# The front of a recurrence unit reordered, and gates computed two units ahead

## The reference, cut to what matters

```python
def step(S, inp):
    w_t, k_t, v_t, kk_t, a_t = inp[:5]
    sa = jnp.einsum('bhvk,bhk->bhv', S, -kk_t)
    S = (S * w_t[:, :, None, :] + sa[..., None] * (kk_t * a_t)[:, :, None, :]
         + v_t[..., None] * k_t[:, :, None, :])
    y = jnp.einsum('bhvk,bhk->bhv', S, inp[5])
```

```python
mu = jnp.mean(wkv, axis=-1, keepdims=True)
var = jnp.mean(jnp.square(wkv - mu), axis=-1, keepdims=True)
gn = ((wkv - mu) * lax.rsqrt(var + GN_EPS)).reshape(B, T, H * N) * ln_g + ln_b
bonus = sum(jnp.sum(r * k_d * r_k, axis=-1, keepdims=True) for k_d in k_dirs) * v
out = (gn + bonus.reshape(B, T, H * N)) * g
```

## Time and profile before

| | us |
|---|---|
| median of 3 runs | 4013.6 (4007.03 to 4015.18) |
| profiled execution, its own time | 4013.55 |
| its span | 4011.7 |
| TensorE busy | 3545.7 (88%) |
| VectorE busy | 1615.0 (40%) |
| ScalarE busy | 1021.3 (25%) |
| GpSimd busy | 1036.3 (26%) |
| mean granted TensorE clock | 0.919 |

### The profile page before, as it was taken

The page is one execution under the profiler, slowest core; times in us unless marked ns, Lnnn a source line. Parts: engine busy times, 40 slices in busy tenths (PEclk is TensorE's granted clock), DMA queues, the critical chain, the costliest instruction groups (busy, mean ns, idle before and its releaser), DMA issues.

```text
span 4011.7 us, 76327 instructions
## 1 busy us (share of the span) xinstructions
PE 3545.7 (88%) x33290; PEld 2603.9 (65%) x33290; DVE 1615.0 (40%) x2806; ACT 1021.3 (25%) x1590; POOL 1036.3 (26%) x664
## 2 busy tenths in 40 slices
PE   8997698879878899989999989859999999979997
PEld 3454477623325677768888855428888888857885
DVE  3255641311126755434333340305555555623333
ACT  2032232211114244331111021312333333223221
POOL 0002341121213200033222120015444444324441
PEclk9997899889988999989999989978889989989998
DMA  4206143169971100111111113420000000012221
GB/s 174 94 32 280 60 181 156 75 258 357 372 280 37 43 1 1 51 77 74 64 63 64 64 59 128 170 93 3 13 13 14 13 14 14 3 64 78 101 95 42
DMA packets 64569, 378.85 MB, mean 94 GB/s; under 512 B 12906, under 2 KB 12906, under 8 KB 26352
## 3 DMA queue, kind: packets, MB, share of 16 engines
q1 hardware_dynamic: 40032, 291.52, 18.7%
q0 software_dynamic: 20608, 68.82, 4.5%
q10 hardware_dynamic: 3600, 13.63, 0.9%
HBM read 380.21 MB, written 44.04 MB: 106 GB/s over the span
## 4 chain that ended last, share of the span: by engine, by line
PE 75%; DVE 10%; DMA 6%; ACT 4%; issue 3%; POOL 2%; SPq 0%; DVEq 0%; ACTq 0%; POOLq 0%
PE psum L462 20%; PE psum L474 11%; PE psum L475 10%; PE psum L476 10%; PE psum L750 4%; DMA arena<-in_wall 3%; PE psum L2096 2%; DVE arena L3146 2%; PE psum L769 2%; PE psum L2123 2%; DMA ring<-in_wall 1%; PE psum L648 1%; PE psum L2814 1%; PE psum L2797 1%; DVE arena L3364 1%
## 5 line engine op out<-in xcount | busy, mean ns | idle before, releaser
L462 PE MATMUL psum<-arena 64*64 64x64 f32 (+3 forms) x13256 | 623.2, 241 | 58.9 <-POOL arena L3049 21.2
L462 PEld LDWEIGHTS psum<-arena 64*64 64x64 f32 (+2 forms) x13256 | 501.1, 143 | 161.9 <-issue 116.5
L492 POOL TENSOR_TENSOR ring_low<-ring,slab_high 128x2048 fp32r<-128x2048 f32 x66 | 303.9, 4618 | 647.5 <-ACT slab_high L485 647.3
L474 PE MATMUL psum<-h_high,slab_high 128*128 128x512 f32 (+1 forms) x1056 | 378.2, 358 | 16.5 <-DVE h_low L512 10.0
L475 PE MATMUL psum<-h_low,slab_high 128*128 128x512 f32 (+1 forms) x1056 | 377.0, 357 | 0.0
L476 PE MATMUL psum<-h_high,ring_low 128*128 128x512 f32 (+1 forms) x1056 | 376.5, 357 | 0.0
L462 PE MATMUL psum<-arena,ring 128*128 128x512 f32 (+3 forms) x992 | 370.4, 533 | 1.8 <-DVEq L1269 1.0
L462 PEld LDWEIGHTS psum<-arena,ring 128*128 128x128 f32 (+2 forms) x992 | 184.8, 187 | 185.4 <-issue 174.9
L941 DVE TENSOR_TENSOR arena<-arena,psum 128x512 f32<-128x512 f32 x66 | 39.5, 599 | 486.1 <-PE psum L476 481.9
L474 PEld LDWEIGHTS psum<-h_high,slab_high 128*128 128x128 f32 x1056 | 201.3, 191 | 51.8 <-issue 10.7
L476 PEld LDWEIGHTS psum<-h_high,ring_low 128*128 128x128 f32 x1056 | 201.6, 191 | 28.5
(11 more groups left out here) (433 smaller groups left out, 6116.0 us busy)
## 6 DMA issues: line engine op xcount, KB each, us to landing
ring<-in_wall SPq DMA_DIRECT2D x181, 1024.0 KB, 5.1
arena<-in_wall SPq DMA_DIRECT2D x96, 1024.0 KB, 12.0
moe_rows<-arena POOLq DMA_DIRECT2D x2, 6144.0 KB, 67.5
arena<-moe_rows ACTq DMA_DIRECT2D x24, 512.0 KB, 7.6
moe_out<-arena POOLq DMA_DIRECT2D x24, 512.0 KB, 9.0
arena<-spill POOLq DMA_DIRECT2D x8, 1024.0 KB, 5.2
spill<-arena POOLq DMA_DIRECT2D x2, 3072.0 KB, 17.6
filters<-arena POOLq DMA_DIRECT2D x2, 2048.0 KB, 6.6
```

Source lines behind the costliest of these rows:

```text
L462: last = L.eng.matmul(out, a, b, start=(i == 0), stop=(i == len(pairs) - 1))
L474: L.eng.matmul(out, a_hi, b_hi, start=(i == 0), stop=False)
L492: L.eng.tensor_tensor(m.low[:, n % SLOTS, :], m.ring[:, n % SLOTS, :], m.high_of(n).bitcast(F32), ALU.subtract).then_inc(m.sem("slab_split ...
```

## The change

- `around` also gives `later`, unit n + 2. Its gates, products and sigmoids, are issued in unit n: on TensorE behind the solved values and ahead of the features products, on ScalarE behind the copies of the solved values. The gates of unit 1 are issued ahead of unit 0. `sigmoid_ready_scalar`, one sigmoid of a single column, stands ahead of those copies.
- A chain step stands behind each operand's six transposes, three in all, and the readout of the states behind the first of the two akv groups.
- The readout of the pair before moves behind corner products: mean in the first level, sums of squares in the second, bonus in the third, turn and gate in the fourth. VectorE centres in the first level, takes the reciprocal in the second, scales in the fourth and ends in the fifth. `readout_tensor` is parted into `readout_sums_tensor` and `readout_bonus_tensor`, and VectorE's bonus product, now `readout_bonus_vector`, stands right behind the scan.
- VectorE's reciprocal of the removal norm moves behind the first chain step of the turns, its two transposes of the inverse ahead of the states' readout.

```diff
-def unit_tensor(L, m, B, u, before, done, after, w2, g2):
-    if after is not None:
-        gates_tensor(L, m, B, after, w2)
+def unit_tensor(L, m, B, u, before, done, after, later, w2, g2):
...
     for k, src in enumerate((u.al, u.be, u.ka)):
-        for half, tiles in enumerate(TURNS):
+        for tiles in TURNS:
             turned.append(turn_pair_tensor(L, m, src, tiles))
-            if before is not None and k < 2:
-                chain_tensor(L, m, B, before, FIRST + 2 * k + half)
-    if done is not None:
-        readout_mean_tensor(L, m, B)
+        if before is not None:
+            chain_tensor(L, m, B, before, FIRST + k)
...
     for hh in range(2):
         L.eng.wait_ge(*akt[hh])
         turned.append(squares_tensor(L, hh, lambda *at: [(square(B.akt, *at), tok(B.vtok, *at))]))
-    if done is not None:
-        readout_tensor(L, m, B, done, g2)
+        if before is not None and hh == 0:
+            chain_tensor(L, m, B, before, ALLCH - 1)
...
         if done is not None and lv == LEVELS[0]:
+            readout_mean_tensor(L, m, B)
+        if done is not None and lv == LEVELS[1]:
+            readout_sums_tensor(L, m, B)
+        if done is not None and lv == LEVELS[2]:
+            readout_bonus_tensor(L, m, done)
+        if done is not None and lv == LEVELS[3]:
             readout_turn_tensor(L, m, B)
-        if done is not None and lv == LEVELS[1]:
             readout_gate_tensor(L, m, B, done, g2)
...
         solved.append(squares_tensor(L, hh, lambda *at: [(square(B.tt, *at), square(B.akv, *at))]))
+    if later is not None:
+        gates_tensor(L, m, B, later, w2)
     for solution in solved:
         L.eng.wait_ge(*solution)
```

ScalarE:

```diff
+def sigmoid_ready_scalar(L, m):
+
+    L.eng.activation(m.stat[:, 20:21], m.tab("gn_eps"), ACT.Sigmoid).then_inc(L.step, 1)
+    L.eng.wait_ge(L.step, L.next_step())
...
-    if after is not None:
-        gates_scalar(L, m, B, after)
...
         if done is not None and lv == LEVELS[0]:
+            L.next_bank()
+            readout_squares_scalar(L, m, B)
+        if done is not None and lv == LEVELS[1]:
+            readout_root_scalar(L, m, B)
+        if done is not None and lv == LEVELS[2]:
             readout_spread_scalar(L, m, B)
...
     if after is not None:
         decay_exp_scalar(L, m, B, after)
+    if later is not None:
+        sigmoid_ready_scalar(L, m)
     for hh in range(2):
         for dst in (B.ua, B.uv):
             ps = L.next_bank()
             L.eng.wait_ge(L.bank_full, L.fill)
             copy(of_head(dst, hh), tiled(ps[:, :TT * CH]), -1.0)
+    if later is not None:
+        gates_scalar(L, m, B, later)
```

VectorE:

```diff
+        chain(FIRST + k)
+        if k == 0 and after is not None and after.d == 0:
+            removal_inverse_vector(L, m, removal_rooted)
     turned_back = []
     for hh in range(2):
         L.eng.wait_ge(m.sem("inverse_begun"), L.nth("inverse_begun"))
         turned_back.append(inverse_turn_vector(L, m, B.ti, B.tt, hh))
-    if after is not None and after.d == 0:
-        removal_inverse_vector(L, m, removal_rooted)
+    L.next_bank()
+    chain(ALLCH - 1)
+    L.next_bank()
     if after is not None:
         decay_scan_vector(L, m, B, after)
     if done is not None:
-        readout_centre_vector(L, m, B, done)
-    L.next_bank()
-    L.next_bank()
-    if done is not None:
-        readout_inverse_vector(L, m, B)
-        bonus = L.next_bank(), L.bank_full, L.fill, L.bank_free, L.read_out
+        readout_bonus_vector(L, m, done)
...
         if done is not None and lv == LEVELS[0]:
+            readout_centre_vector(L, m, B)
+        if done is not None and lv == LEVELS[1]:
+            readout_inverse_vector(L, m, B)
+        if done is not None and lv == LEVELS[2]:
+            bonus = L.next_bank(), L.bank_full, L.fill, L.bank_free, L.read_out
+        if done is not None and lv == LEVELS[3]:
             terms = readout_scale_vector(L, m, B, done, bonus)
-        if done is not None and lv == LEVELS[1]:
-            readout_vector(L, m, B, done, terms)
+            gate = L.next_bank(), L.bank_full, L.fill, L.bank_free, L.read_out
+        if done is not None and lv == LEVELS[4]:
+            readout_vector(L, m, B, done, terms, gate)
```

More of the change, by code:

```diff
@@ L3256, in unit_scalar @@
         copy(of_head(B.akv, hh), tiled(ps[:, :TT * CH]), 1.0)
-    if done is not None:
-        readout_root_scalar(L, m, B)
+        if before is not None and hh == 0:
+            L.next_bank()
     if after is not None and after.d == 0:
@@ L3277, in unit_scalar, with unit_vector @@
             copy(of_head(dst, hh), tiled(ps[:, :TT * CH]), -1.0)
+    if later is not None:
+        gates_scalar(L, m, B, later)
     for _ in range(8):
         L.next_bank()
-def unit_vector(L, m, B, u, before, done, after):
+def unit_vector(L, m, B, u, before, done, after, later):
     e = L.eng
@@ L3328, in unit_vector @@
     for k in range(3):
-        for half in range(2):
-            L.next_bank()
-            if k < 2:
-                chain(FIRST + 2 * k + half)
+        L.next_bank()
+        L.next_bank()
+        chain(FIRST + k)
+        if k == 0 and after is not None and after.d == 0:
+            removal_inverse_vector(L, m, removal_rooted)
     turned_back = []
@@ L3369, in unit_vector @@
         L.next_bank()
+    if later is not None:
+        L.next_bank(2)
+        L.next_bank(2)
     ecol = u.ecol.rearrange("q (t p) -> q t p", p=2)
@@ L3404, in readout_tensor @@
         L.eng.wait_ge(bank_free, count)
-    L.eng.matmul(ps, ones, u.bk, start=True, stop=True).then_inc(L.bank_full, 1)
+    L.eng.matmul(ps, m.tab("heads64"), u.bk, start=True, stop=True).then_inc(L.bank_full, 1)
 def readout_gate_tensor(L, m, B, u, g2):
@@ L3492, in around @@
     u = unit(n)
[L3493 removed]
+    return u, unit(n - 1), (unit(n - 1) if u.d == 0 else None), unit(n + 1), unit(n + 2)
 def recurrence_tensor(L, m, B, w2, g2):
     prepare_tensor(L, m, B, Unit(B, 0), w2)
+    gates_tensor(L, m, B, Unit(B, 1), w2)
     for n in range(UNITS):
@@ L3552, in recurrence_vector @@
     terms = readout_scale_vector(L, m, B, last, bonus)
-    readout_vector(L, m, B, last, terms)
+    gate = L.next_bank(), L.bank_full, L.fill, L.bank_free, L.read_out
+    readout_vector(L, m, B, last, terms, gate)
 def build(nc, a):
```

45 lines of the change are left out of this document (23 added, 22 removed).

## The result

The changed kernel takes 3956.8 us in the median of 4 runs (3951.7 to 3957.6), the kernel before in the same comparison 4011.7: a ratio of 0.9868, 95% interval 0.9848 to 0.9887. The profiled execution has a span of 3955.8 us against 4011.7. The sign was right and so were most of the steps; the size was not, and the term that was most too small is the clock's.

The account below looks back on a forecast made before the run. TensorE was taken as the bound, with only its idle time and clock to win. Waits removed -35.9, new waits +17.5, mask waits -2 and clock -6 gave -26 us: 4013.6 to 3988 us, range 3962 to 4014.

Parts of the forecast that it names:

- Gates: Behind the solved values, units 0 to 13: gates cover TensorE's 0.79 us wait for ScalarE's copies; 11.0 us gained.
- step 2: Scores: TensorE's waits for PSUM banks that gates hold until the sigmoids read them go; 2.5 us of 4.3 gained.
- Readout squares: Readout sums: TensorE's seven waits for ScalarE's square go, as sums stand a level behind the mean; 10.9 us gained.
- spread: Odd units: TensorE's wait for the removal norm's spread goes, as its reciprocal moves up on VectorE; 3.5 us gained.
- Chain in the turns: Turns: six transposes behind every chain step remove hidden waits, 0.55 us a unit; 8 us gained over 15 units.
- Bonus product: First corner level, even units: VectorE's product, issued ahead of GpSimd, takes 0.75 us; TensorE idles 0.35 us for masks.
- Sums in the second level: Second corner level, even units: VectorE stands still for the reciprocal ahead of updates; TensorE idles 0.55 us a unit.
- Last part of readout: Fifth level, even units: two VectorE operations delay the solved values 0.7 us, a GpSimd operand product 0.7 us more.
- The clock: First corner of four even units: the half-speed spell behind the 1.55 us wait goes; 6 us gained.
- the clock steadies: Rival, units 1 to 14: 50 of 132 us at half speed go, another 15 us gained, 3973; chance 0.15.
- the clock takes it back: Rival, turns: runs of transposes lengthen the low stretch 3.4 us in 15 units, 16 us lost, 4009; chance 0.17.
- VectorE as the bound of the even levels: Rival, five levels of seven even units: inserted VectorE operations uncovered, 8.7 us a unit, 4037; chance 0.12.

Follow-up runs that it names:

- gates-alone kernel: Kernel before with only the gates moved two units ahead, chain and readout left in place: ratio 0.9922 to the kernel before.
- chain-alone kernel: Kernel before with only chain steps, states' readout and the removal norm's reciprocal moved: ratio 0.9977 to the kernel before.
- the parts alone: Kernel before with one part of the change each: gates 0.9922, chain 0.9977, readout 0.9988.
- the fourteen kernels: The changed kernel and all follow-up variants, each timed beside the kernel before: ratios 0.9754 to 0.9958.
- with the product added: Changed kernel with three VectorE waits moved (0.9823), plus one unread 128x512 product ahead of the removal norm's twelve narrow sums in odd units: 0.9812.
- without the gates: Changed kernel with the gates put back at the head of the unit before: ratio 0.9950 to the kernel before.
- before with wide sums: Kernel before with the removal norm's twelve narrow sums replaced by one 128x512 product, norm not computed rightly: ratio 0.9958.

## Why the prediction was wrong

By its steps:

- *Gates* (11.0 us): right for the waits listed. L462's wait for ScalarE is 1.6 us in two units instead of 11.8 in fifteen, and in the gates-alone kernel idle time fell by 14.6 us, with the bank waits of step 2 (2.5) in it. At full speed that kernel is 22 us shorter, though: 8 us more lay under modelled ends, which neither step counted.
- *Readout squares* (10.9) and *spread* (3.5): right. Neither wait is in the list after.
- *Chain in the turns* (8 us under modelled ends): right in size. The chain-alone kernel, which has the spread's 3.5 us in it as well, is 12 us shorter at full speed where 11.5 were reckoned. But it was the only step with hidden waits, and in the changed kernel there are some 20 us of them.
- *Bonus product*: right in mechanism. It is issued behind the scan and takes 0.73 us in the median, not 1.87; GpSimd's first copy waits for it (0.63 us where it took 0.2). Mask wait 0.77 us against 0.35 reckoned.
- *Sums in the second level* (0.55): 0.61 measured, by the very path named: sums, table load, reciprocal, update.
- *Last part of readout* (0.7 + 0.7): too small. Over the program L3501 takes 2.126 us in the median and 0.752 at least. The wait for GpSimd was 1.4 us, not a mean of 0.7, in every unit but the tail, since the two engines stand in the same order each time; TensorE lost 2.4 to 2.6 us, not 1.4. A collision in a fixed schedule has no average: it is to be priced by the place where the two meet, or at both ends.
- Together the visible idle time was to fall by 12 us (35.9 - 8 + 2 - 17.5) and fell by 5.9.
- *The clock* (6 us): this is the step that failed. "With the wait gone I count 6 us gained" looked at one stretch in four even units, 14 us at half speed. Between the two traces 82 us went, from 136.6 to 54.6, worth 29 us at 0.35 each; over all executions 57 us, worth 20. I took the long stretches in the front as given and put their shortening into a rival. That rival, "the clock steadies" (50 us more at 0.31 each, 15 us on top of the 6), has both the amount and the price nearly right, and it had a chance of 0.15 only. It gave 3973. Of the 16 us from there to 3957, 8 are waits that no step had, 2 the lower median of the kernel before in this comparison, and 6 lie within the interval of the ratio.

Forecast and result side by side, units 1 to 14 (the same sum from the other side):

| | forecast | in the two traces |
|---|---|---|
| visible idle time | -12 | -6 |
| waits under modelled ends | -8 | -22 |
| clock | -6 | -29 |
| sum | -26 | -57 |

With the half-speed time of all executions the clock's line is -20 and the sum -48, where the ratio says -53 (interval -61 to -45). Which waits beside the chain's lay under modelled ends stays open: none is long enough to be listed, and no run parted them further.

The rival by which the clock takes it back is refuted: half-speed time fell, and the front of unit 6 runs its longest row of transposes at 1.00. The Trainium skill, TensorE: Matmul & The Clock Gate ("Part 4: PE-mode transpose"), says that transpose-mode matmuls don't count as busy time for the clock gate in the same way. If so, it was no bar here: twelve of them in a row, 1.53 us amid chain steps and scores without waits, didn't lower the clock. VectorE as the bound of the even levels did not come either, but its price shows: (21.6 + 5.4) / 7 = 3.9 us of new waits in an even unit, of the 5.4 at which it would have decided, and the even units gained less than the odd ones. That the readout's move is worth nothing by itself (0.9988 alone, 0.9880 without it against 0.9868 with it) is this rival's share.

## What to carry to other kernels

Where TensorE is 93% busy, look at the granted clock of the stretch beside its idle time: small waits and narrow products cost once by their length and again by the half-speed stretch that follows. Price a us at half speed from units of one kernel that do the same work (0.35 us here), not from two kernels that also differ in waits. And before crediting a change with a steadier clock, take the mean clock of all executions: one trace of the kernel before was 31 us off the mean of 58. Price what would be left if the stretch had no lull, not only the lull that one sees end in a slow matmul. Two engines whose order is fixed meet at the same point each time: look up which instruction holds the other there.

## What the runs showed that I had not expected

- The three traces of the parts alone each show some 40 us less at half speed than the trace before; over all executions the gates take 29 us off, the readout 5 and the chain none. Most of what the traces showed was the before trace's own excess.
- Length at full speed plus 0.35 x half-speed time of all executions gives the gain of each of the fourteen kernels within 6 us.
- One 1.1 us product in place of twelve narrow instructions in every second unit brought TensorE's clock to 1.00 over 624 us of the profiled execution (0.9823 to 0.9754).
- Work added in a lull can be free: 4 matmul instructions more in each of seven units of the changed kernel left its ratio at 0.9869 (0.9868 without them).
- VectorE's product of two SBUF operands, issued 0.23 us behind a GpSimd product of 1.81 us, took 2.12 us instead of 0.75. The Trainium skill, SBUF — State Buffer (section "SBUF: two separate sides"), has this as an exclusive port pair that the first holds for its whole instruction; both signs of it are in this trace, L3501 longer behind GpSimd's product and GpSimd's copy of 12 columns 0.63 us behind L3481, where it takes 0.20 in the odd units.
- The long stretches of 7 to 20 us at half speed that come up at the end of single even units (unit 4 before, unit 8 with the product added, one each without the gates and before with wide sums) stand behind a short idle time of TensorE amid the features products, which no semaphore ended ("issue"); the clock falls 1.3 to 2.4 us after it:

```profile
2954.48 5.81 PE L462 MATMUL psum<-arena 64*64 64x64 f32 x135 [0.86 <-issue]
3118.15 4.15 PE L462 MATMUL psum<-arena 64*64 64x64 f32 x101 [1.14 <-issue]
```

  (the kernel before and the one with the product added). In all fifteen traces such idle times of over 0.7 us come eleven times in units 1 to 14. Four have a stretch behind them, of 0.86, 0.93, 1.10 and 1.14 us; the seven others are 0.72 to 0.90 us long and have none. What holds the issue up stays open. It comes in other units in each trace, and so is part of what makes one execution differ from the next.
